# A mixer, its queries and its expert rows: running the second block's latents by tiles of 128 instead of both tiles at once

## The chip, the core and the metric

The kernel runs on one core of one Trainium2 chip. All data is float32. The metric is the device time of one execution in microseconds (us); lower is better. The engines are TensorE (PE, with its weight loads as PEld), VectorE (DVE), ScalarE (ACT), GpSimd (POOL) and SyncE (SP), each with a queue of its own that runs in order.

## What is computed

Two transformer blocks run one after the other on 256 tokens of width 1024, two tiles of 128 tokens. The second takes the first one's output as its "latents" and has 256 context tokens beside them (tiles 2 and 3). It has two layers: an even one (latent attention with 8 heads over context and latents, and a short convolution) and an odd one (4 heads of an mLSTM). After either mixer stands a layer of looked-up experts:

```python
def peer(h, w_q, subkeys, u, v):            # for each block of 128 tokens
    q = (xb @ w_q).reshape(128, 8, 2, 128)   # w_q: 1024 x 2048
    s = einsum('thpd,hpkd->thpk', q, subkeys)
    s1, i1 = top_k(s[:, :, 0], 16); s2, i2 = top_k(s[:, :, 1], 16)
    top, pos = top_k(all 256 sums of s1 and s2, 16); idx = i1 * 128 + i2 at pos
    g = softmax(top)
    ue, ve = u[idx], v[idx]                  # 8 heads x 16 rows of u and of v for every token
    return einsum('thk,thkd->td', g * gelu(einsum('td,thkd->thk', xb, ue)), ve)

# layer: x += gate * mixer(norm1(x)); x += gate * peer(norm2(x))
# layer 0 for context and latents, layer 1 for the latents alone
```

## The kernel before

Everything is written by hand: each engine has a program, a chain of Python generators, and waits on events of the others. What a program text says first, the engine does first.

**Expert rows.** For one tile, 128 times (8 heads by 16 picks) a row `x` is gathered: POOL issues one indirect DMA (L2111) that fetches, for each of 128 tokens, 2048 floats (a row of u and one of v), 1 MB. The tile pair makes 256 such rows. A row then passes DVE (the dot product with the token's normed vector, L2059), ACT (the gelu, a pair of rows at a time, L2024), DVE again (a diagonal matrix of the weights, L2054) and PE (four instructions of 128x512, L2012), and its buffer is free: only then may POOL issue the row that takes the buffer next. The text calls this the row's loop. There are three passes of 256 rows: the context's ("c", beside the first block and the latents' even mixer), the latents' of layer 0 ("l0") and of layer 1 ("l1"). The two latent passes have 11 buffers. DVE, in its spare time between dots, does the top sixteens: three instructions of them for every row (`rate` 3), 29 instructions for each of the 15 head-and-tile units left, so for the first 145 rows.

**Before the rows** stand, for the latents, the queries (`queries_pe`, L1930: weights of 256 columns as stationary blocks, both tiles' 256 tokens streamed past them, 8 pairs of blocks; L1941: the scores against the subkeys, 128 wide) and before them a norm and the mixer's tail: attention units and the output projection (L690), whose result DVE and POOL add to x (L1383, L1391). In layer 0 the tail has 16 units (8 heads by 2 tiles) and runs beside the end of the context's rows, and rows of layer 1's modulation (`more`; L324, L326, L339 on DVE, 16 pieces of 512 KB) are computed beside the queries. In layer 1 the tail has 8 units (4 heads by 2 tiles) and runs alone.

**Merging.** `merged(a, b)` advances two generators by declared shares: after a step of `a` with share s, steps of `b` with share `ROW` (0.47) are made until s is used up. This happens in each engine's program, so it sets one fixed order there.

```python
        def merged(a, b, due=0.0):
            for share in a:
                due += share
                while due > 0.0:
                    due -= next(b, 1.0e9)
            return due
```

Of the kernel before, what the change touches and what calls it, by code (L numbers as in the profile page):

```python
# [118 lines left out]
def program(nc, D, out):  # L119
    with ExitStack() as ctx:  # L120
# [93 lines left out]
        FIRST, SIX, PAIR = {0: (0, 1, 2, 3), 1: (0, 1, 2, 3, 4)}, (0, 1, 2, 3, 4, 5), (6, 7)  # L214
        BESIDE, SUMS = (4, 5, 6), (5, 6)
# [633 lines left out]
        CH, ROW, PACE = 0.45, 0.47, 0.8  # L849
# [576 lines left out]
        units2 = [(h, i) for h in range(8) for i in range(2)]  # L1426
# [5 lines left out]
        RINGS = {"c": BESIDE, "l": FIRST[1]}  # L1432

# [8 lines left out]
        def even_pe(pe, side):  # L1442
# [33 lines left out]
            for _ in lin_pe(pe, ("ukv", side), D["mla_w_ukv_2"][0], 1, (0, 1024), keys,  # L1476
                            lambda kc, t: kv_lhs(kc, t, tiles), seen=seen, ring=ring):
                pe.fill(1, side)
                yield CH
            nk = len(keys)  # L1480

            def s1(u):
                h, i = units2[u]
                if i == 0:
                    for n, src, m in (("q", b.Qh, 2), ("k", b.Kh, nk)):
                        flip_pe(pe, ("e" + n, side, h), [src[:, x, h, :] for x in range(m)], ring, ("rope2", side),
                                ("kr", side), [("ev", "lin", "uq", side, x, c) for x in tiles for c in (0, 512)],
                                [("ev", "lin", "ukv", side, x, c) for x in keys for c in (0, 512)])
                bk = bank(pe, ring, "esc", side, u)
                pe.wait_ge(("ev", "flip", "eq", side, h), ("ev", "flip", "ek", side, h))  # L1490
                pe.eng.matmul(bk[:, 0:128 * nk], b.QTE[h % 2][0:96, i * 128:(i + 1) * 128], b.KTE[h % 2][0:96, 0:128 * nk],
                              start=True, stop=True).then_inc(*pe.done("mm", "esc", side, u))

            def s2(u):
                bk = bank(pe, ring, "ept", side, u)
                pe.wait_ge(("ev", "esc", side, u))
                for x in range(nk):
                    ins = pe.eng.transpose(bk[:, x * 128:(x + 1) * 128], b.PB[u % 2][:, x * 128:(x + 1) * 128], ident)
                ins.then_inc(*pe.done("mm", "ept", side, u))

            def s3(u):
                h, i = units2[u]
                bk = bank(pe, ring, "eav", side, u)
                pe.wait_ge(("ev", "ept", side, u))
# [3 lines left out]
                ins.then_inc(*pe.done("mm", "eav", side, u))  # L1508

            for _ in stages(16, s1, s2, s3):  # L1510
                yield 0.5
            for t in tiles:
                turn_pe(pe, ("eo", side, t), b.O2[:, t - tiles[0], :], 4, ring,
                        [("eo", side, u) for u in range(16) if units2[u][1] == t - tiles[0]])
            seen = {t: turned_all(("eo", side, t), 4) + [("cy", side, 3)] for t in tiles}
            for _ in lin_pe(pe, ("eout", side), D["even_w_out_2"][0], 8, (0, 1024), tiles,
# [6 lines left out]
        def even_sp(sp, side):  # L1523
# [6 lines left out]
            for _ in range(18):  # L1530
# [8 lines left out]
        def even_act(a, side):  # L1539
# [49 lines left out]

            def s1(u):  # L1590
                h, i = units2[u]
                if i == 0:
                    copy_act(a, b.QTE[h % 2][0:96, :], psum("flip", "eq", side, h)[0:96, 0:256], ("mm", "flip", "eq", side, h),
                             ("mm", "esc", side, u - 3)).then_inc(*a.done("ev", "flip", "eq", side, h))
                a.wait_ge(a.last, ("enm", side, u), ("mm", "ept", side, u - 2))
                a.eng.activation(b.PB[u % 2][:, 0:128 * nk], psum("esc", side, u)[:, 0:128 * nk], ACT.Exp,
                                 bias=sm(1, "enm", u % 4), scale=96.0 ** -0.5, accum_out=sm(1, "esu", u % 4)).then_inc(
                    *a.done("ev", "esc", side, u))
# [1039 lines left out]
```

## Time and profile before

| | |
|---|---|
| median of 3 runs | 3900.23 us (3899.17 to 3910.28) |
| the profiled execution | 3910.66 us, span of its instructions 3909.4 us |
| PE busy | 3081.3 us, 79% of the span |
| DVE busy | 2423.5 us, 62% |
| POOL busy | 943.3 us, 24% |
| ACT busy | 809.2 us, 21% |
| moved by DMA | 1102 MB, mean 282 GB/s; of it 818.9 MB by the 768 gathers |
| mean granted clock of PE | 0.903 of 2.4 GHz |

The span can be read in stretches. Up to about 1990 us the first block, the context's whole layer 0 and the latents' even mixer run beside one another. From 1990 to 2125 us stand norm and queries of l0, then its 256 rows to about 2795 us. Then come the odd mixer's projections to 3001 us, its attention units to 3104 us, its output projection and norm to 3161 us, the queries of l1 to 3229 us, and its rows to the end.

### The profile page before, as it was taken

How to read it: one execution, taken by the hardware profiler on the slowest of the kernel's cores; microseconds unless marked ns; L12 is line 12 of the kernel's file. 1: busy time of each engine (PE TensorE's matmuls, PEld its weight loads, DVE VectorE, ACT ScalarE, POOL GpSimd, SP SyncE). 2: the span in 40 equal slices, each digit the busy share in tenths (PEclk: the TensorE clock that was granted, in tenths of full speed). 3: DMA queues.
4: the chain of work that ended last, by engine and by line, in shares of the span. 5: the costliest groups of instructions: out<-in, count | busy, mean ns of one | idle time of the engine just before them, and what ended most of it. 6: DMA issues, size and time to landing. Idle time of an engine off the chain costs nothing. (4 is left out here: it accounts for less than half of the span.)

```text
span 3909.4 us, 28560 instructions
## 1 busy us (share of the span) xinstructions
PE 3081.3 (79%) x8865; PEld 1611.0 (41%) x8865; DVE 2423.5 (62%) x5350; ACT 809.2 (21%) x1912; POOL 943.3 (24%) x842
## 2 busy tenths in 40 slices
PE   6899797899784689978777777777797796777776
PEld 1354464674332347635444222322343362222322
DVE  3124525886778856545655999866513518999665
ACT  1102232232323433223511111100101211111000
POOL 0000101222222222222211344433200014444432
PEclk7999898999896789989788999999996698999999
DMA  6665236999885679977555999999743039999998
GB/s 231 198 181 170 85 112 216 334 347 358 298 325 191 231 276 362 357 288 273 192 185 188 421 405 392 382 421 422 294 126 131 4 115 394 412 387 377 422 421 352
DMA packets 299625, 1102.17 MB, mean 282 GB/s; under 512 B 25588, under 2 KB 110272, under 8 KB 201168
## 3 DMA queue, kind: packets, MB, share of 16 engines
q0 software_dynamic: 114512, 818.87, 53.2%
q1 hardware_dynamic: 184336, 280.90, 21.7%
q8 instruction: 70, 1.15, 0.1%
q10 hardware_dynamic: 624, 0.57, 0.1%
q14 instruction: 83, 0.68, 0.0%
HBM read 1099.18 MB, written 1.05 MB: 281 GB/s over the span
## 5 line engine op out<-in xcount | busy, mean ns | idle before, releaser
L2012 PE MATMUL PS<-AR 128*128 128x512 f32 x2560 | 1256.2, 635 | 453.1 <-DVE AR L2054 351.9
L2111 POOL DMA_INDIRECT AR<-in_uv,AR x768 | 865.2, 1127 | 1713.4 <-PE PS L2012 1251.1
L2059 DVE CUSTOM_DVE_ANT_0 AR<-AR 128x1024 f32<-128x1024 f32 x768 | 935.4, 1220 | 293.8 <-DMA AR<-in_uv,AR 293.3
L2012 PEld LDWEIGHTS PS<-AR 128*128 128x128 f32 x2560 | 490.9, 200 | 1166.9 <-DVE AR L2054 546.0
L690 PE MATMUL PS<-AR 128*128 128x512 f32 (+3 forms) x1304 | 564.2, 587 | 37.0 <-DMA AR<-in_w_in 19.8
L2024 ACT ACTIVATE AR<-AR 128x2 f32<-128x2 f32 x384 | 78.1, 203 | 1479.7 <-DVE AR L2059 1478.7
L690 PEld LDWEIGHTS PS<-AR 128*128 128x128 f32 x1304 | 249.3, 204 | 324.7 <-issue 269.8
L326 DVE SCALAR_TENSOR_TENSOR AR<-AR,CC 128x512 f32<-128x512 f32 x280 | 210.5, 752 | 220.1 <-DMA AR<-in_w_ada 138.6
L987 PE MATMUL PS<-AR 128*128 128x256 f32 x1408 | 325.2, 390 | 21.9 <-DMA AR<-in_w_up_act 14.8
L987 PEld LDWEIGHTS PS<-AR 128*128 128x128 f32 x1408 | 274.5, 196 | 86.7 <-issue 20.6
L1930 PE MATMUL PS<-AR 128*128 128x256 f32 x768 | 189.2, 409 | 25.7 <-DMA AR<-in_peer_w_q 18.6
L2054 DVE TENSOR_SCALAR AR<-C,AR 128x128 f32<-128x128 f32 x512 | 156.6, 376 | 66.4 <-DVE AR L2059 48.6
L2024 ACT ACT_TABLE_LOAD x90 | 115.5, 1283 | 370.5 <-DVE AR L2059 370.5
L746 ACT ACTIVATE AR<-PS 128x256 f32<-128x256 f32 (+4 forms) x244 | 107.9, 442 | 372.8 <-PE PS L1930 160.1
L1930 PEld LDWEIGHTS PS<-AR 128*128 128x128 f32 x768 | 157.3, 208 | 52.4 <-DMA AR<-in_peer_w_q 19.4
L2047 DVE SCALAR_TENSOR_TENSOR AR<-AR 128x1024 f32<-128x1024 f32 x126 | 163.9, 1301 | 13.0 <-ACT AR L2035 8.6
L1001 PE MATMUL PS<-AR 128*128 128x512 f32 x352 | 154.7, 592 | 1.1 <-DVE AR L1221 1.1
L545 PE MATMUL PS<-C,AR 128*128 128x128 f32 x254 | 54.6, 385 | 114.9 <-DVE AR L629 65.4
L443 PE MATMUL PS<-AR,CC 128*2 128x512 f32 x192 | 93.1, 641 | 21.3 <-DMA AR<-in_w_mod 15.3
L1391 POOL TENSOR_TENSOR X<-X,AR 128x512 f32<-128x512 f32 x12 | 16.0, 1339 | 357.6 <-DVE AR L1383 357.6
L1001 PEld LDWEIGHTS PS<-AR 128*128 128x128 f32 x352 | 66.8, 190 | 85.6 <-issue 83.5
L545 PEld LDWEIGHTS PS<-C,AR 128*128 128x128 f32 x254 | 44.0, 201 | 132.1 <-DVE AR L629 66.1
(226 smaller groups left out, 2518.9 us busy)
## 6 DMA issues: line engine op xcount, KB each, us to landing
AR<-in_w_mod SPq DMA_DIRECT2D x96, 512.0 KB, 4.7
AR<-in_w_ada SPq DMA_DIRECT2D x96, 512.0 KB, 4.8
AR<-in_w_in SPq DMA_DIRECT2D x56, 512.0 KB, 4.1
AR<-in_peer_w_q SPq DMA_DIRECT2D x48, 512.0 KB, 3.5
AR<-in_w_up_act SPq DMA_DIRECT2D x44, 512.0 KB, 8.2
AR<-in_w_up_lin SPq DMA_DIRECT2D x44, 512.0 KB, 6.4
AR<-in_w_down SPq DMA_DIRECT2D x44, 512.0 KB, 6.6
AR<-in_even_w_in SPq DMA_DIRECT2D x24, 512.0 KB, 4.8
```

The lines of the kernel that those rows point to most:

```text
L326: v.eng.scalar_tensor_tensor(out=acc, in0=wt[:, c, :], scalar=col, in1=acc, op0=ALU.mult, op1=ALU.add).then_inc(*v.done(*end))
L690: ins = pe.eng.matmul(bk[:, 0:n], lhs(k0 + kc, t), wt[:, kc, :], start=(k0 + kc == 0), stop=(k0 + kc == nk - 1))
L746: return a.wait_ge(a.last, *events).activation(dst, src, ACT.Copy)
L987: ins = pe.eng.matmul(bk[:, f * 256:f * 256 + 256], wt[:, kc, cs], LAT.all[:, k0 + kc, :], start=(k0 + kc == 0 and f == 0), stop=(k0 + kc ...
L1001: ins = pe.eng.matmul(bs[t, hh], GT[:, f, t * 128:(t + 1) * 128], wt[:, 0, hh * 512:(hh + 1) * 512], start=(f == 0), stop=(f == 21))
L1930: ins = pe.eng.matmul(bk[:, f * 256:f * 256 + 256], wt[:, kc, cs], e.lay.all[:, k0 + kc, :], start=(k0 + kc == 0 and f == 0), stop=(k0 + k ...
L2012: ins = pe.eng.matmul(acc[i][hh], e.dg(x), e.buf(x)[:, 1024 + 512 * hh:1536 + 512 * hh], start=(x % 128 == 0), stop=(x % 128 == e.last))
L2024: a.eng.activation(hid, hid, ACT.Gelu).then_inc(*a.done("gelu2", e.key, x // 2))
L2047: v.eng.scalar_tensor_tensor(out=ACC, in0=row, scalar=w, in1=ACC, op0=ALU.mult, op1=ALU.add).then_inc(*v.done("sum", e.key, x))
L2054: v.eng.tensor_scalar(e.dg(x), ident, DT[x // 128][:, x % 128:x % 128 + 1], gw_at(x // 16, x % 16, 1), ALU.mult, ALU.mult).then_inc(*v.don ...
L2059: v.eng.tensor_tensor_reduce(e.buf(x)[:, 0:1024], e.buf(x)[:, 0:1024], norm2(e).H[e.tiles[x // 128]], 1.0, 0.0, ALU.mult, ALU.add, DT[x // ...
L2111: g.eng.indirect_dma_start(e.buf(x), None, D["uv"][e.l], bass.IndirectOffsetOnAxis(ap=idx_at(x // 16, x % 16, 1), axis=0)).then_inc(*land. ...
```

## The change

The latents of the second block no longer go through tail, queries and rows as a pair.

- The mixers' tails are functions of their own and take one tile: `even_tail_*(lane, "l0")` or `"l1"` with 8 units each, `odd_tail_*(lane, t)` with 4 units each. In both, a unit turns its head's keys anew: with two tiles apart every unit has its own key transposes and key copy.
- `queries` takes a list of tiles. For the latents it is run once for tile 0 and once for tile 1, so that the 8 MB of `peer_w_q` are read twice in each layer, and PE streams 128 tokens past each stationary block instead of 256.
- `second` sets the order: queries of tile 0, then the rows start; merged with them come tile 1's tail and tile 1's queries. In layer 0, `more` runs after that, one piece for each row.
- The row buffers: six until row 80, eleven after that. Tile 1's tail and queries use the memory of the other five.
- The sums of the rows have two PSUM banks (5, 6) instead of a ring of seven, so tile 1's first sum waits until tile 0's banks are read. The tails and queries have the rings (0 to 4), (0 to 3) and (4, 7).
- `ROW` is 0.45 instead of 0.47.
- The norm after the mixer is made for each tile by itself; for both tiles its shift is now added on DVE, where POOL had added tile 1's.

```diff
-        CH, ROW, PACE = 0.45, 0.47, 0.8
+        CH, ROW, PACE = 0.45, 0.45, 0.8
...
+        def query_tiles(e, ts):
+            w = 128 * len(ts)
+            base = ACC if ts[0] == 1 else SMALL[:, 768:1280]
+            return w, [base[:, w * i:w * i + w] for i in range(2)]
...
                             for kc in range(4):
-                                ins = pe.eng.matmul(bk[:, f * 256:f * 256 + 256], wt[:, kc, cs], e.lay.all[:, k0 + kc, :],
+                                ins = pe.eng.matmul(bk[:, f * w:f * w + w], wt[:, kc, cs], e.lay.all[:, k0 + kc, cols],
...
         def experts_pool(g, e):
-            g.wait_ge(("mm", "sco", e.key, 15), e.ready)
+            g.wait_ge(("mm", "sco", e.key, e.tiles[0], 15), e.ready)
             for st in range(e.steps):
                 if st < 256:
                     x, b = st, e.before[st]
                     g.wait_ge(("idx", e.key, x // 16), ("sum", e.key, b) if b is not None else None)
+                    if b is None and e.slot[x] in e.late:
+                        g.wait_ge(e.late_ready)
...
+        def odd_tail_pe(pe, t):
             def s1(u):
-                h, t = units3[u]
-                if t == 0:
-                    flip_pe(pe, ("oq", h), [Qp[:, i, h * 128:(h + 1) * 128] for i in range(2)], SIX,
-                            [("ev", "lin", "oq", x, 0) for x in range(2)])
-                    flip_pe(pe, ("ok", h), [Kp[:, i, h * 128:(h + 1) * 128] for i in FOUR], SIX,
-                            [("ev", "lin", "ok", x, 512) for x in FOUR])
-                bk = bank(pe, PAIR, "osc", u)
+                h = u % 4
+                flip_pe(pe, ("oq", u), [Qp[:, t, h * 128:(h + 1) * 128]], QUAD, [("ev", "lin", "oq", x, 0) for x in range(2)])
+                flip_pe(pe, ("ok", u), [Kp[:, i, h * 128:(h + 1) * 128] for i in FOUR], QUAD,
+                        [("ev", "lin", "ok", x, 512) for x in FOUR])
+                bk = bank(pe, LAST, "osc", u)
...
+        def staged(t, *parts):
+            for _ in stages(4, *[(lambda u, f=f: f(4 * t + u)) for f in parts]):
+                yield 1.5
...
-        WIDE = [0, 1, 2, 3, 4, 5, 8, 9, 10, 11, 12]
-        of_lat = [Experts(f"l{l}", l, [0, 1], LAT, 3, MAIN, HTt[:, 0:1024], WIDE, 0, 3, MAIN,
-                          mods.finished() + [("sum", before, 255)])
-                  for l, mods, before in ((0, more, "c"), (1, mods_of["odd"], "l0"))]
+        of_lat = [Experts(f"l{l}", l, [0, 1], LAT, 3, SUMS, HTt[:, 2048:3072], list(range(6)), 0, 3, FIRST[1], ready,
+                          [[0], [1]], late=[8, 9, 10, 11, 12], since=80, late_ready=after)
+                  for l, ready, after in ((0, [("sum", "c", 255)], res_x(("eout", "l1"), 1)),
+                                          (1, mods_of["odd"].finished() + [("sum", "l0", 255)], res_x(("oout", 1), 1)))]
...
+        def second(lane, l, tail, queries, experts, mods=None):
+            through(queries(lane, of_lat[l], [0]))
+            rows = experts(lane, of_lat[l])
+            merged(tail(lane, 1), rows)
+            merged(queries(lane, of_lat[l], [1]), rows)
+            lane.run(mods, "rows")
+            for _ in rows:
+                lane.fill(1, "rows")
+            lane.flush("rows")
...
-            merged(even(lane, "l"), beside, due)
+            due = merged(even(lane, "l"), beside, due)
+            merged(tail(lane, "l0"), beside, due)
             through(beside)
-            lane.run(more, "l0")
-            through(queries(lane, of_lat[0]))
-            lane.flush("l0")
+            second(lane, 0, lambda lane, t: tail(lane, f"l{t}"), queries, experts, more)
...
         def pe_program(pe):
             start_pe(pe)
-            both(pe, first_pe, even_pe, queries_pe, experts_pe)
-            through(experts_pe(pe, of_lat[0]))
+            both(pe, first_pe, even_pe, even_tail_pe, queries_pe, experts_pe)
             odd_pe(pe)
-            through(queries_pe(pe, of_lat[1]))
-            through(experts_pe(pe, of_lat[1]))
+            through(odd_tail_pe(pe, 0))
+            second(pe, 1, odd_tail_pe, queries_pe, experts_pe)
```

Three places of the order show what it does. On PE, at the queries of l1, the program had the queries of both tiles (L1930 256 wide; L1941 the scores) and, after the last of them, all sums of the rows (L2012):

```order
L1930 MATMUL PS<-AR 128x256 x16
L1941 MATMUL PS<-AR 128x128 x4
L1930 MATMUL PS<-AR 128x256 x16
L1941 MATMUL PS<-AR 128x128 x6
L2012 MATMUL PS<-AR 128x512 x512
```

In the changed kernel the second tile's queries (L1970, scores L1981) stand between the row sums (L2053, two of its matmuls for a row), here in layer 0 right behind the norm's transposes (L545):

```order
L545 MATMUL PS<-C,AR 128x128 x8
L1970 MATMUL PS<-AR 128x128 x16
L2053 MATMUL PS<-AR 128x512 x6
L1981 MATMUL PS<-AR 128x128
L2053 MATMUL PS<-AR 128x512 x4
L1970 MATMUL PS<-AR 128x128 x16
L1981 MATMUL PS<-AR 128x128
L2053 MATMUL PS<-AR 128x512 x4
L1981 MATMUL PS<-AR 128x128
L2053 MATMUL PS<-AR 128x512 x4
```

So each block of 16 query matmuls now stands behind four or five rows' sums, and the next sums stand behind it. On POOL, in layer 1, the residual sums (L1391), the subkey loads (L1994) and the gathers (L2111) were:

```order
L1391 TENSOR_TENSOR X<-X,AR 128x512 x4
L636 TENSOR_TENSOR AR<-AR,MOD 128x1024
L1994 DMA AR<-in_subk 128x4x128 x4
L2111 DMA AR<-in_uv,AR 128x2048 x256
```

and are now, with the subkey loads at L2035 and the gathers at L2153:

```order
L1391 TENSOR_TENSOR X<-X,AR 128x512 x2
L2035 DMA AR<-in_subk 128x4x128 x4
L2153 DMA AR<-in_uv,AR 128x2048 x28
L1391 TENSOR_TENSOR X<-X,AR 128x512
L2153 DMA AR<-in_uv,AR 128x2048 x4
L1391 TENSOR_TENSOR X<-X,AR 128x512
L2153 DMA AR<-in_uv,AR 128x2048 x2
L2035 DMA AR<-in_subk 128x4x128
L2153 DMA AR<-in_uv,AR 128x2048 x9
```

Two residual sums have come between the gathers, and each waits for a product that DVE makes behind the dots of the rows before. On DVE, the pieces of `more` in layer 0 (L324, L326), which stood beside the queries, are now between the dots (L2100), the diagonals (L2095) and the top sixteens (L1847 to L1916) of rows from about the sixtieth on:

```order
L326 SCALAR_TENSOR_TENSOR AR<-AR,CC 128x512 x4
L2095 TENSOR_SCALAR AR<-C,AR 128x128 x2
L2100 ISA AR<-AR 128x1024
L2100 ISA AR 128x1
L1856 MAX AR<-AR 128x8
L1859 MAX_INDEX AR<-AR 128x8
L1886 TENSOR_SCALAR AR<-AR 128x16
L326 SCALAR_TENSOR_TENSOR AR<-AR,CC 128x512 x4
```

One piece of four instructions has moved behind each row's dot and top sixteens.

## Rows read from the trace of the kernel before

**Rows 1.** The page, 40 equal slices of the span: busy tenths of DVE and DMA

```profile
DVE  3124525886778856545655999866513518999665
...
DMA  6665236999885679977555999999743039999998
```

**Rows 2.** Windows, busy time of each engine (instructions), granted clock, DMA share, GB/s

```profile
1855.00:1950.00 95.00, 67.00 (x292) 44.89 (x291) 60.74 (x119) 51.98 (x99) 23.29 (x18) 0.78 0.54 185
1990.00:2125.00 135.00, 99.37 (x373) 72.67 (x371) 70.72 (x117) 18.57 (x44) 7.10 (x8) 0.84 0.40 128
2125.00:2510.00 385.00, 277.66 (x557) 108.85 (x556) 353.66 (x969) 60.38 (x135) 166.17 (x149) 0.92 0.98 396
2510.00:2795.00 285.00, 217.35 (x470) 85.08 (x468) 176.05 (x346) 14.72 (x63) 105.95 (x109) 0.99 0.98 408
3001.00:3104.00 103.00, 78.29 (x168) 39.42 (x166) 58.52 (x172) 29.15 (x63) 0.00 (x0) 0.61 0.00 1
3104.00:3161.00 57.00, 37.09 (x97) 19.21 (x98) 16.44 (x25) 9.08 (x28) 8.89 (x7) 0.79 0.26 81
3161.00:3229.00 68.00, 66.37 (x320) 57.28 (x320) 9.30 (x34) 12.54 (x32) 1.54 (x3) 0.98 0.32 102
3229.00:3610.00 381.00, 273.08 (x547) 107.26 (x548) 350.81 (x963) 59.74 (x134) 166.79 (x147) 0.92 0.98 397
3610.00:3885.00 275.00, 208.53 (x455) 82.04 (x454) 173.18 (x341) 11.59 (x57) 108.27 (x111) 1.00 1.01 421
```

**Rows 3.** Timeline of POOL: first and last gather of l0, first of l1

```profile
2125.39 1.00 POOL L2111 DMA_INDIRECT AR<-in_uv,AR  x1 [25.79 <-PE PS L1941]
...
2769.22 0.94 POOL L2111 DMA_INDIRECT AR<-in_uv,AR  x1 [2.80 <-PE PS L2012]
...
3228.95 1.00 POOL L2111 DMA_INDIRECT AR<-in_uv,AR  x1 [25.36 <-PE PS L1941]
```

**Rows 4.** Waits, 2510 to 2780 us: us in total, times, longest

```profile
DVE AR L2059 <- DMA AR<-in_uv,AR: 79.0, 100, 1.3
```

**Rows 5.** Timeline of PE, 3119 to 3179 us: output projection, queries, scores

```profile
3119.62 29.27 PE L690 MATMUL PS<-AR 128*128 128x512 f32 x64
...
3177.48 1.41 PE L1941 MATMUL PS<-AR 128*128 128x128 f32 x8
3178.72 7.07 PE L1930 MATMUL PS<-AR 128*128 128x256 f32 x32
```

**Rows 6.** Weight loads of the l1 queries, 3161 to 3229 us: busy, mean ns

```profile
L1930 PEld LDWEIGHTS PS<-AR 128*128 128x128 f32 x256 | 49.1, 195 | 8.0 <-issue 1.4
```

**Rows 7.** Timeline of PE in l0's rows: the sums of two rows

```profile
2154.69 3.70 PE L2012 MATMUL PS<-AR 128*128 128x512 f32 x8 [2.02 <-DVE AR L2054]
```

**Rows 8.** Waits of DVE in the odd units, 3001 to 3104 us

```profile
DVE AR L2310 <- ACT AR L746: 35.0, 15, 4.8
DVE AR L749 <- PE PS L2185: 3.4, 1, 3.4
DVE AR L749 <- PE PS L574: 1.7, 1, 1.7
```

**Rows 9.** Waits of DVE in the even units, 1855 to 1950 us

```profile
DVE SM L1697 <- PE PS L1491: 23.8, 11, 3.0
```

**Rows 10.** DVE by line, 1990 to 2125 us: the modulation's pieces

```profile
L326 DVE SCALAR_TENSOR_TENSOR AR<-AR,CC 128x512 f32<-128x512 f32 x56 | 42.1, 752 | 7.5 <-DMA AR<-in_w_mod 5.6
L324 DVE TENSOR_SCALAR AR<-AR,CC 128x512 f32<-128x512 f32 x8 | 3.9, 486 | 6.6 <-PE PS L363 6.4
L339 DVE SCALAR_TENSOR_TENSOR MOD<-PS,MOD 128x512 f32<-128x512 f32 x4 | 2.8, 692 | 19.1 <-PE PS L363 19.1
```

**Rows 11.** Timeline of POOL, the odd mixer's residual sums of tile 0

```profile
3134.33 1.26 POOL L1391 TENSOR_TENSOR X<-X,AR 128x512 f32<-128x512 f32 x1 [307.15 <-DVE AR L1383]
```

**Rows 12.** The gathers, 2150 to 2480 us, from issue to landing

```profile
DMA to landing us min/median/max: 5.5/9.3/18.6
```

**Rows 13.** Windows: rows merged with the first block, columns as in rows 2

```profile
1300.00:1850.00 550.00, 473.25 (x1577) 300.37 (x1576) 322.18 (x551) 178.11 (x420) 144.17 (x122) 0.92 0.84 304
```

More of the change, by code:

```diff
@@ L1488, in s1 @@
                                 [("ev", "lin", "ukv", side, x, c) for x in keys for c in (0, 512)])
[L1489 to L1492, printed above, removed]
+                bk = bank(pe, ring, "esc", part, u)
@@ L1494, in s2 @@
+                pe.wait_ge(("ev", "flip", "eq", part, h), ("ev", "flip", "ek", part, h))
+                pe.eng.matmul(bk[:, 0:128 * nk], b.QTE[h % 2][0:96, at(i):at(i) + 128], b.KTE[h % 2][0:96, 0:128 * nk],
+                              start=True, stop=True).then_inc(*pe.done("mm", "esc", part, u))
             def s2(u):
-                bk = bank(pe, ring, "ept", side, u)
-                pe.wait_ge(("ev", "esc", side, u))
+                bk = bank(pe, ring, "ept", part, u)
+                pe.wait_ge(("ev", "esc", part, u))
@@ L1529, in even_sp, with even_tail_sp @@
                     yield CH
-            for _ in range(18):
+        def even_tail_sp(sp, part):
+            side = part[0]
+            for _ in range(len(UNITS[part]) + 2):
                 yield 0.5
@@ L1766, in program, with __init__ @@
         class Experts:
-            def __init__(self, key, l, tiles, lay, gate, banks, tmp, early, lag, rate, ring, ready, halved=False):
+            def __init__(self, key, l, tiles, lay, gate, banks, tmp, early, lag, rate, ring, ready, parts, halved=False, late=(), since=256,
+                         late_ready=()):
+                self.parts, self.late, self.late_ready = parts, late, list(late_ready)
                 self.halved = halved
@@ L1785, in __init__, with part, scored @@
                 self.slot, self.before, last_in = {}, {}, {}
-                free = list(early)
                 for x in range(256):
+                    free = list(early) + (list(late) if x >= since else [])
                     fresh = [i for i in free if i not in last_in]
-                    i = fresh[0] if fresh and x >= len(early) else (
-                        free[x] if x < len(early) else min(free, key=lambda i: last_in[i]))
+                    i = fresh[0] if fresh else min(free, key=lambda i: last_in[i])
                     self.slot[x], self.before[x] = i, last_in.get(i)
                     last_in[i] = x
+            def part(self, t):
+                return next(ts for ts in self.parts if t in ts)
+            def scored(self, t, u):
+                return ("ev", "sco", self.key, self.part(t)[0], u)
             def on_dve(self, x):
@@ L2081, in experts_dve @@
             todo = topk_all(v, e, 1, 16)
-            v.wait_ge([("ev", "sco", e.key, u) for u in range(16)])
             for st in range(e.steps):
@@ L2204, in odd_sp, with odd_tail_sp @@
             sp.flush()
-            for _ in lin(sp, 8, (0, 1024), [0, 1], nothing):
-                pass
+        def odd_tail_sp(sp, t):
+            yield from staged(t, nothing, nothing, nothing, nothing)
+            for _ in lin(sp, 8, (0, 1024), [t], nothing):
+                yield CH
+            yield 1.0
         def odd_act(a):
@@ L2493, in context @@
                 yield PACE * share
+            for share in tail(lane, "c"):
+                yield PACE * share
             lane.run(cgate, "c")
-            for share in queries(lane, of_ctx):
+            for share in queries(lane, of_ctx, [2, 3]):
                 yield PACE * share
@@ L2498, in context, with both @@
             yield from experts(lane, of_ctx)
-        def both(lane, first, even, queries, experts):
-            beside = context(lane, even, queries, experts)
+        def second(lane, l, tail, queries, experts, mods=None):
[7 more added lines that the diff above has]
+            lane.flush("rows")
+        def both(lane, first, even, tail, queries, experts):
+            beside = context(lane, even, tail, queries, experts)
             due = merged(first(lane, 0), beside)
```

364 lines of the change are left out of this document (189 added, 175 removed).

## The prediction

> **What bounds the kernel now.** I read the slices first [rows 1]: DMA is full in slices 22 to 29 and 33 to 40, the two latent passes, and nearly idle at slices 31 to 33, the odd mixer's tail. The windows give each stretch its limit [rows 2]. A pass has two parts. In the first 145 rows DVE also does the top sixteens: l0 takes 385 us, of which about 12 us are the start, so 373/145 = 2.57 us a row, with DVE busy 353.7 us (2.44 a row) and DMA at 0.98. DVE and DMA are both at their limit. In the other 111 rows DVE is busy 62% and PE 76%, DMA alone sets the pace at 2.5 us a row, and DVE waits for it 100 times [rows 4]. In l1 the same numbers return. Between the passes stand stretches in which no row moves: 1990 to 2125 us, and 3001 to 3229 us. The gathers start at 2125.4 and 3229.0 us [rows 3].
>
> The change shortens these stretches and puts what it takes out into the first 62 rows of each pass. (Tile 1's tail and queries declare shares of 9.6 and 18 in layer 0, 9 to 11 and 18 in layer 1; over 0.45 this is about 20 and 40 rows, of which the order shows 61 or 62.) Those rows are the ones where DVE has nothing to spare. So the question is how much DVE time was idle in what is removed, and how much new waiting DVE gets.
>
> **What is removed from in front of the rows.**
>
> Layer 1. Attention: 8 units took 103 us [rows 2]; four take four steps of about 12 and the same filling and draining, some 60: −43. Output projection: 64 instructions in 29.3 us [rows 5], half of it −15. Scaling and squares of four heads fewer: −3. Queries: a pair of blocks took 7.07 + 1.41 us [rows 5]. For 128 tokens the nearest row is the score's, the same shape with a stationary block of its own: 8 instructions in 1.41 us, 0.176 each. A pair is then 32 + 4 of them, 6.3 us, not half of 8.5: the weight loads, 195 ns [rows 6], no longer hide behind a stream of 221 ns. Eight pairs and 2 us around them make 52 us for 68: −16. Sum −77.
>
> Layer 0. The tail runs beside the last context rows. Its step took 95/16 = 5.9 us with one row in it [rows 2]; ten steps for 18, each now with key transposes and a key copy, say 6.5: −35. Projection and residual −10. The new `ROW` moves ten context rows ahead, into a stretch where PE is busy 86% [rows 13]; I charge 15. Norm and queries took 135 us with `more` beside them, now 14 + 52: −69. Sum −99.
>
> Together **−176**.
>
> **What is added to the rows.**
>
> Queries of tile 1, in either layer: PE does 40 rows at 1.85 [rows 7] and 8 pairs at 6.3, 125 us. Rows merged with other PE work kept PE busy 86% [rows 13], so 145 us where 40 rows took 103: +42 each. If PE were never idle it would be +22; that is the lower bound.
>
> Layer 1's tail: DVE's work for four units is 58.5/2 = 29, two key copies 1.4, and the norm side half of 16.4 plus a shift of 1.2 that POOL did: +40 in all [rows 2]. DVE's waits come along, since its queue is in order and dots stand behind them. In each unit it waits for ACT's copy of a PSUM bank that PE fills only after DVE's own key copy: 35.0/2 = 17, draining 5 [rows 8]; root of the squares, transposes and norm, estimated from the same stretch's idle DVE, 8. The two residual sums are new waits on POOL: it holds the next gathers until DVE has made the product [rows 11], so DVE finds no landed row and waits out 1.3 us of adding and 5.5 us of the shortest landing [rows 12], 7 each: 14. Sum +84.
>
> Layer 0's tail: 10 steps with 11 rows in them. The step of before plus a key flip and a whole row's sum on PE instead of half is 7.5: 75 us for 28, +47. DVE's waits there were for scores, up to 3.0 us each [rows 9]. Projection: PE 14.6 + 8 rows of 1.85 = 29, at 86% 34 us for 21: +13. Residual sums beyond that +7, norm +7. Sum +74.
>
> `more`: 42.1 + 3.9 + 2.8 = 49 us of DVE [rows 10]. It was hidden beside the queries, where DVE was half idle. Now it stands behind rows 62 to 79, which still carry top sixteens, so all of it counts: +49. Spread over the last 111 rows it would have cost nothing.
>
> Small ones: sums of tile 1 wait for tile 0's banks, +4 a pass; the 12 us start of a pass is in part covered, −5 a pass; DMA carries some 16 MB more, in rows where it now has room, 0. After a wait DVE finds rows landed and works at 2.44 instead of 2.57: 124 rows by 0.13, −16.
>
> Sum: layer 1 84 + 42 − 1 = 125; layer 0 74 + 42 + 49 − 1 = 164; less 16: **+273**. Against −176 this is +97, on the profiled execution's 3910.7 us 4008; the median of the runs was 10 us below it: **3997, say 4000 us**.
>
> **Rivals.**
>
> 1. *It overlaps as meant.* No waits of DVE beyond its work: layer 1's tail +40, layer 0's about +30 (60.7 us of DVE there over 16 steps, less its rows), queries +22 each, `more` +49, less 16: +147 against −176, **3871 us**. For it: PE is a few us ahead of DVE at each step's start, since the last diagonal is one to two rows old. Against it: the ACT waits of [rows 8] arise from DVE's own copy, so no lead helps. It decides at one number: with `more` fixed at 49, the rows 0 to 61 of both passes may take (176 − 49)/124 = 1.02 us more than 2.57, so below 3.6 us a row the kernel is faster. I expect 4.4. Chance 0.12.
>
> 2. *The six buffers set the pace.* A row's loop is issue 1, landing 5.5, its dot and three top sixteens 2.4, the partner's dot and diagonals 2.2, the sum 1.85: 13 us, over 6 buffers 2.2 us a row, under 2.57. But each block of 5.6 us on PE and each wait of DVE lies in the loop once or twice; where both do, 6 rows take over 30 us, 5.2 a row. Over 124 rows that is 0.8 us a row more than forecast, **4100 us**. The median landing of 9.3 us [rows 12] speaks for it, though there 11 buffers queue up. Chance 0.13.
>
> 3. *Nothing measurable*, between 1 and the forecast, **3900 us**: the units' waits fall where rows are late anyway. Chance 0.07.
>
> 4. *The narrow query matmuls cost half.* If 16 of them took 7.07/2 us, a pair would be 4.2: 2.1 less, 33 us over the serial 16 pairs and about 40 over the merged ones, **3927 us**. Against it stands the score's row at the same width, 0.176 a piece. Chance 0.03. The Trainium skill goes further: its page "TensorE: Matmul & The Clock Gate", section "Back-to-back issue gap", gives some 81 ns for a pair of weight load and 128-wide matmul, and "LDWEIGHTS (loading the stationary operand)" 107 ns for 128 columns. By that the pair of blocks would be 2.9 us and the kernel would come out near 3865. This trace does not agree for float32: 176 ns between instructions, 195 ns for a load.
>
> The forecast itself, a slower kernel by some 60 to 150 us, has 0.65.
>
> **How the numbers follow.** A measurement of this kernel tells about 0.3% (12 us) from no change. Faster: rival 1 and a little of 4, 0.13. Same: 0.08. Slower: the rest, 0.79. The range goes from the sum without any waiting, 3875, up to rival 2's, 4100: 3875 to 4100 leaves out some 0.15. The forecast's own range is 3950 to 4060.
>
> **What would show it.** The first gather of l0 near 2030 us, that of l1 some 151 us behind the start of the odd units instead of 228. Then 60 rows at 4 to 4.6 us each, with DMA at 0.6 and DVE at 0.75; DVE waiting for ACT copies, for PE's scores and, at two places in a pass, 7 us for a gather. In the queries' rows PE busy 85% or more and each 16 matmuls near 5.6 us. In l0's rows 62 to 79, 5.3 us a row. From row 145 on 2.5 us as before. A first stretch under 3.6 us a row would make the prediction wrong; so would `more` running beside landed rows without lengthening them, or query matmuls of 0.11 us.

## The result

| | median (lowest to highest, runs) |
|---|---|
| before | 3905.26 us (3899.17 to 3912.38, 4) |
| after | 3963.67 us (3961.41 to 3978.71, 4) |

The ratio is 1.0157, with a 95% interval of 1.0124 to 1.019: the change makes the kernel 58 us slower. The profiled execution of after took 3978.71 us, 68 more than that of before and 15 above after's median, so the two executions read below differ by 10 us more than the medians do. The slices of after's page, each 99 us, against [rows 1]:

```profile
span 3977.4 us, 29933 instructions
DVE  3124426896768756554556888866513376799665
PEclk7999898999986789989788969999996778999999
DMA  6665236998985689977568969999733357999998
```

The l0 pass now begins in slice 21, but with 6 and 8 tenths of DMA, and has a hole (6 tenths) in slice 24; l1 begins in slice 33 with 5 and 7. Windows of after, in the order of the program (rows with tail, with queries, with `more`, the last 111 rows; then l1's tail and queries). Columns as in [rows 2]:

```profile
2011.00:2134.00 123.00, 83.93 (x261) 44.53 (x259) 77.77 (x202) 32.08 (x62) 31.63 (x28) 0.81 0.67 245
2134.00:2274.00 140.00, 116.11 (x461) 69.87 (x462) 107.79 (x286) 29.70 (x77) 51.80 (x46) 0.92 0.94 367
2274.00:2393.00 119.00, 78.61 (x99) 25.75 (x99) 93.99 (x193) 9.96 (x21) 24.71 (x21) 0.67 0.69 264
2560.00:2835.00 275.00, 207.29 (x448) 81.05 (x447) 169.86 (x333) 11.19 (x55) 102.27 (x105) 0.99 1.00 417
3187.00:3372.00 185.00, 118.01 (x267) 54.05 (x268) 128.18 (x344) 42.60 (x91) 43.49 (x40) 0.79 0.65 237
3372.00:3501.00 129.00, 110.91 (x448) 66.14 (x448) 103.59 (x279) 25.71 (x69) 44.54 (x43) 0.94 0.96 372
```

In the tail's rows no engine is near its limit (DVE 63 and 69%, DMA 0.67 and 0.65): they are rows of waits. With the queries DMA is at 0.94 to 0.96 and PE at 83 and 86%. With `more` DVE is busy 79% and DMA a third idle. The last rows are as before.

The balance, by the times between the dots of two rows. Gain: the first dot of l0 stands at 2017.6 us instead of 2131.0, −113.4, and from l0's last dot to l1's first it is 363.8 us instead of 445.5, −81.7; −195 in all. Loss: l0's pass takes 817.2 instead of 658.2 us (+159), l1's 761.8 instead of 657.7 (+104); +263. The difference is the +68.

This table is worked out from the timelines: us from the dot of one row to that of another, for all kernels. The first number is l0's, the second l1's; a pass goes from the dot of row 0 to that of row 255.

| kernel | rows 0–34 | 34–62 | 62–80 | 80–145 | 145–255 | pass |
|---|---|---|---|---|---|---|
| before | 93, 92 | 77, 77 | 49, 49 | 167, 167 | 273, 273 | 658, 658 |
| after | 165, 173 | 91, 95 | 119, 52 | 167, 167 | 274, 275 | 817, 762 |
| e1 | 167, 173 | 91, 96 | 49, 51 | 167, 167 | 294, 275 | 768, 762 |
| e2 | 167, 175 | 92, 95 | 116, 54 | 155, 162 | 277, 277 | 806, 764 |
| e3 | 89, 90 | 68, 67 | 46, 46 | 164, 164 | 277, 277 | 644, 644 |
| e4 | 111, 113 | 82, 80 | 50, 50 | 222, 167 | 266, 275 | 731, 685 |
| e5 | 98, 97 | 79, 79 | 50, 51 | 167, 167 | 272, 273 | 666, 667 |
| e6 | 160, 179 | 94, 92 | 119, 50 | 167, 167 | 275, 275 | 814, 763 |
| e7 | 157, 164 | 90, 96 | 119, 51 | 167, 167 | 274, 275 | 807, 753 |
| e8 | 150, 166 | 92, 96 | 43, 43 | 160, 157 | 302, 277 | 748, 740 |
| e9 | 166, 174 | 86, 90 | 119, 51 | 167, 167 | 274, 275 | 812, 757 |
| e10 | 143, 162 | 74, 77 | 46, 43 | 164, 161 | 303, 277 | 729, 720 |
| e11 | 135, 138 | 98, 108 | 74, 73 | 157, 156 | 297, 276 | 760, 750 |

The first dot of l0 stands between 2003 and 2031 us in the kernels whose program is the same up to there, so single profiles differ by up to 28 us ahead of the rows; where that matters, the passes are compared. Within a pass, rows 0 to 22 of l1 took 100.8 us in after and 104.2 and 104.3 in e6 and e2, whose edits begin later: 3 us in one cell of the table is no difference.

### The profile page after: what moved, and what is told of

It reads as the page before. It is cut to its first block and busy times, and to the rows that moved or that the text cites. A ratio compares the mean times of both kernels' runs of the same rounds, so it can differ in the third digit from the quotient of the medians.

```text
span 3977.4 us, 29933 instructions
## 1 busy us (share of the span) xinstructions
PE 3119.6 (78%) x9425; PEld 1652.0 (42%) x9425; DVE 2443.9 (61%) x5365; ACT 832.1 (21%) x1999; POOL 951.1 (24%) x848
## 5 line engine op out<-in xcount | busy, mean ns | idle before, releaser
L2053 PE MATMUL PS<-AR 128*128 128x512 f32 x2560 | 1274.8, 641 | 381.0 <-DVE AR L2095 294.4
L2153 POOL DMA_INDIRECT AR<-in_uv,AR x768 | 870.9, 1134 | 1862.1 <-PE PS L2053 1383.9
L2100 DVE CUSTOM_DVE_ANT_0 AR<-AR 128x1024 f32<-128x1024 f32 x768 | 936.1, 1222 | 353.9 <-DMA AR<-in_uv,AR 352.7
L2053 PEld LDWEIGHTS PS<-AR 128*128 128x128 f32 x2560 | 499.1, 204 | 1076.3 <-issue 495.6
L690 PE MATMUL PS<-AR 128*128 128x512 f32 (+3 forms) x1304 | 575.5, 593 | 46.3 <-DMA AR<-in_w_in 20.0
L690 PEld LDWEIGHTS PS<-AR 128*128 128x128 f32 x1304 | 252.0, 207 | 339.0 <-issue 281.0
L326 DVE SCALAR_TENSOR_TENSOR AR<-AR,CC 128x512 f32<-128x512 f32 x280 | 210.6, 752 | 217.1 <-DMA AR<-in_w_ada 138.3
L987 PE MATMUL PS<-AR 128*128 128x256 f32 x1408 | 324.7, 389 | 17.2 <-DMA AR<-in_w_up_act 12.2
L987 PEld LDWEIGHTS PS<-AR 128*128 128x128 f32 x1408 | 273.2, 195 | 84.0 <-issue 21.3
L2095 DVE TENSOR_SCALAR AR<-C,AR 128x128 f32<-128x128 f32 x512 | 161.2, 382 | 76.1 <-DVE AR L2100 48.3
L1970 PE MATMUL PS<-AR 128*128 128x128 f32 (+1 forms) x1280 | 193.2, 313 | 11.0 <-ACT AR L746 3.8
L746 ACT ACTIVATE AR<-PS 128x128 f32<-128x128 f32 (+6 forms) x316 | 120.2, 380 | 360.6 <-PE PS L1970 142.6
L545 PE MATMUL PS<-C,AR 128*128 128x128 f32 x254 | 53.4, 377 | 179.3 <-DVE AR L629 124.2
L1970 PEld LDWEIGHTS PS<-AR 128*128 128x128 f32 x1280 | 180.5, 206 | 29.0 <-issue 12.5
L1001 PE MATMUL PS<-AR 128*128 128x512 f32 x352 | 154.7, 592 | 1.1 <-DVE AR L1221 1.1
L545 PEld LDWEIGHTS PS<-C,AR 128*128 128x128 f32 x254 | 42.7, 196 | 196.5 <-DVE AR L629 133.0
L1001 PEld LDWEIGHTS PS<-AR 128*128 128x128 f32 x352 | 66.8, 190 | 85.2 <-issue 83.5
L1391 POOL TENSOR_TENSOR X<-X,AR 128x512 f32<-128x512 f32 x12 | 16.2, 1354 | 342.8 <-DVE AR L1383 342.8
```

The costliest lines, as they stand in the source:

```text
L326: v.eng.scalar_tensor_tensor(out=acc, in0=wt[:, c, :], scalar=col, in1=acc, op0=ALU.mult, op1=ALU.add).then_inc(*v.done(*end))
L690: ins = pe.eng.matmul(bk[:, 0:n], lhs(k0 + kc, t), wt[:, kc, :], start=(k0 + kc == 0), stop=(k0 + kc == nk - 1))
L746: return a.wait_ge(a.last, *events).activation(dst, src, ACT.Copy)
L987: ins = pe.eng.matmul(bk[:, f * 256:f * 256 + 256], wt[:, kc, cs], LAT.all[:, k0 + kc, :], start=(k0 + kc == 0 and f == 0), stop=(k0 + kc ...
L1001: ins = pe.eng.matmul(bs[t, hh], GT[:, f, t * 128:(t + 1) * 128], wt[:, 0, hh * 512:(hh + 1) * 512], start=(f == 0), stop=(f == 21))
L1970: ins = pe.eng.matmul(bk[:, f * w:f * w + w], wt[:, kc, cs], e.lay.all[:, k0 + kc, cols], start=(k0 + kc == 0 and f == 0), stop=(k0 + kc = ...
```

## The experiments

Ratios are to runs of the kernel before on the same chip, with a 95% interval. "After" is the changed kernel.

**e1: `more` one piece to every fourth row, in rows 154 to 214** (`st` counts the rows left behind the queries, 62 fewer than the row's number).

```diff
-            for _ in rows:
-                lane.fill(1, "rows")
+            for st, _ in enumerate(rows):
+                if st >= 92 and st % 4 == 0:
+                    lane.fill(1, "rows")
```

> The changed kernel, but in layer 0 the 16 pieces of the modulation `more` are computed beside rows of the last part of the pass, one piece for every fourth row from about row 155 on, instead of one for each of the rows 62 to 79. Theory A (DVE has nothing to spare in the first 145 rows, and has 0.9 us a row to spare in the last 111): the rows 62 to 80 of layer 0, which took 119 us against 49 in the kernel before, go back to about 49, and the last part of the pass grows by under 10 us; the kernel is 60 to 70 us faster than the changed one, about 3900, as fast as the kernel before or a little faster. Theory B (the slow rows 62 to 80 come from the six row buffers and not from the pieces): these rows stay near 110 us, and the time stays within 15 us of the changed kernel's 3964.

Measured: 3929.28 us, ratio 1.0056 [1.0038, 1.0075], 34 us under after in the median and 48 in the profile, where theory A has 60 to 70. Rows 62 to 80 fell from 119 to 49 us, the time of before: `more` had cost 70 there, more than the 49 of the sum. So A is right there, and B is wrong. But rows 145 to 255 took 294 us, 20 more and not the under 10 of theory A. Windows of e1, at rows 62 on and in the last rows:

```profile
2340.00:2395.00 55.00, 39.31 (x82) 15.54 (x83) 51.69 (x143) 9.38 (x21) 21.70 (x21) 0.97 1.01 421
2560.00:2700.00 140.00, 111.52 (x230) 43.33 (x229) 110.29 (x202) 7.47 (x29) 59.84 (x50) 0.95 1.02 418
```

DVE is busy 79% in the last rows and hides `more`; DMA is at 1.02. The pieces are 16 of 512 KB, 8.4 MB, and at 421 GB/s they take 20 us. Here work moved into rows that wait for DMA was free on DVE, not in bytes.

**e2 and e3: two top-sixteen steps in a row instead of three, from row 24,** in after (e2) and in before (e3).

```diff
+            def pace(self, st):
+                return 2 if not self.halved and st >= 24 else self.rate
-                for _ in range(e.rate):
+                for _ in range(e.pace(st)):
```

> The changed kernel, but both latent passes do three instructions of the top sixteens a row only for the first 24 rows and two a row after that. Theory A (DVE bounds the merged rows and those up to 145): each row from 24 to 145 gives back up to 0.34 us of DVE, so merged rows and the rows up to 145 get faster until DMA at 2.5 us a row bounds them: 10 to 25 us a pass, 3915 to 3945. The rows 145 to 205 carry the rest of the top sixteens in DVE's spare time and stay at 2.5 us. Theory C (waits for other engines and not DVE's work bound the merged rows): under 10 us in all, 3955 to 3965.

> The kernel before with the same slower pace of the top sixteens. Theory A: the rows 24 to 145 go from 2.57 to DMA's 2.5 us, so 5 to 10 us a pass, 3880 to 3895. If DMA alone had been the bound there, no change.

Measured: e2 3973.07 us, 1.0165 [1.0133, 1.0196], no gain; e3 3881.43 us, 0.9944 [0.9923, 0.9965], 22 us less than before. In before, rows 34 to 62 fell from 77 to 68 us, 2.43 a row, so DVE's work had been above DMA's there (theory A, with more than its 5 to 10 us a pass: 14). In after the same rows stayed at 92: with a third less top sixteens they are not shorter, so the work of DVE was not alone in setting them. Rows 80 to 145 of e2's l0 did get faster, by 12 us; in l1 by 5.

**e4: e1 with tile 1's tail and queries run ahead of the rows, still in parts of one tile.**

```diff
-            merged(tail(lane, 1), rows)
-            merged(queries(lane, of_lat[l], [1]), rows)
+            through(tail(lane, 1))
+            through(queries(lane, of_lat[l], [1]))
```

> The changed kernel with the late modulation of e1_more_late, and with tile 1's tail and queries in front of the rows, not merged with them: only the split by tiles is left, and all the rows run undisturbed. Against e1: the passes should take some 640 us again (86 us less in layer 0, 104 us less in layer 1), and in front of the rows the tile's tail and queries stand alone, some 110 to 130 us in each layer. Theory A: 25 to 70 us slower than e1, about 3925 to 3970, so the merging itself gains a little and what it gains is smaller than the 200 us that it hides, because DVE's and PE's work comes back in the rows. Theory D (the merging loses): this kernel is faster than e1.

Measured: 4031.8 us, 1.0335 [1.0304, 1.0365], 103 over e1. The first dot of l0 comes 93 us later than in e1, and l1's gap grows by 120 us (484 for 364). The merging itself wins: 213 us of serial time for 115 us of rows (l1's pass falls by 77, l0's by 38). Of these 98 us some 27 are not the merging's: with no rows used up ahead of it, the same line puts `more` into rows 92 to 152, beside top sixteens, and rows 80 to 255 take 488 us for e1's 461. Theory A had the direction, and 25 to 70 us for the measured 103. What is lost against before is the splitting: l1's gap in e4 is 38 us longer than before's 445.5, and rows 0 to 34 take 111 and 113 us instead of 93. The trace shows why these rows are slower. The gathers may start when tile 0's scores are in, so the first six go out before the last query weights of tile 1 (l0 of e4, PE, then DVE's waits over rows 1 to 34, in both layers the same 17.0 us):

```profile
2119.42 3.53 PE L1970 MATMUL PS<-AR 128*128 128x128 f32 x16 [8.56 <-DMA AR<-in_peer_w_q]
2126.27 3.52 PE L1970 MATMUL PS<-AR 128*128 128x128 f32 x16 [3.31 <-DMA AR<-in_peer_w_q]
...
DVE AR L2095 <- ACT AR L2065: 17.9, 2, 17.0
```

PE waits for the weights, ACT's copy of the scores waits for PE, the gelu of the first row pair stands behind it, and DVE waits 17.0 us for that. Six buffers add 5 (e5); together this is the 19 to 20 us.

**e5 and e6: the six buffers.** e5 is before, with its rows up to 80 on six buffers; e6 is after, with the other buffers from row 24 (l0) and 36 (l1) instead of 80, and this is its edit:

```diff
-                          [[0], [1]], late=[8, 9, 10, 11, 12], since=80, late_ready=after)
+                          [[0], [1]], late=[8, 9, 10, 11, 12], since=(24, 36)[l], late_ready=after)
```

> The kernel before, but both latent passes use only six row buffers until row 80, as the changed one does; nothing is merged with the rows. Theory E (the six buffers by themselves slow the rows, apart from what is merged): as in the unmerged passes of e4_serial, the rows 0 to 80 take about 243 us instead of 218, so 25 us a pass and 50 us in all, 3945 to 3960. Theory F (a row's loop of 13 us over six buffers is short enough, and e4's slower start had another cause): under 15 us in all, up to 3918.

> The changed kernel, but the five later row buffers are used from row 24 on in layer 0 and from row 36 on in layer 1, right behind tile 1's tail, instead of from row 80 on. Theory E: the rows from there to 80 are the queries' rows, which cost 20 to 24 us more a pass than before; with eleven buffers they give back 10 to 20 us a pass, so 3925 to 3945, and rows 62 to 80 of layer 0 change too. Theory F: PE's query matmuls and DVE's waits for other engines set the pace there whatever the buffers are; under 10 us in all, 3954 to 3964.

Measured: e5 3931.78 us, 1.007 [1.0048, 1.0092], +28; e6 3969.77 us, 1.017 [1.0142, 1.0199], the same as after. In e5 the passes grow by 8 and 10 us, all of it in rows 0 to 74, about 0.12 us a row: neither E's 25 a pass nor F's under 15 in all. Of the 28 us, 5 lie outside the passes in the profile and 5 are the difference between medians and profiled executions; no run says more of them. DVE's waits over the first 156 us of e5's pass:

```profile
DVE AR L2060 <- DMA AR<-in_uv,AR: 9.6, 13, 4.4
```

It waits 13 times for a row: 4.4 us at the first one, 5.2 in the other 12. Before has 5.5 us in 2 such waits there. In e6 rows 22 to 34 of l0 gain 6 us and rows 34 to 62 lose 3; the passes are the same within 3 us (theory F). Six buffers cost something, and not what a pass loses. The two PSUM banks for the sums cost no more: e4, which has them, takes 82 and 80 us for rows 34 to 62, e5, which has seven, 79 and 79.

**e7: the two residual sums beside the rows made by DVE itself instead of POOL.**

```diff
+                if key in BESIDE_ROWS:
+                    v.wait_ge(v.last)
+                    v.eng.tensor_tensor(Xt[:, t, c0:c0 + n], Xt[:, t, c0:c0 + n], res_tmp(tmp, i), ALU.add).then_inc(
+                        *v.done("summed", *key, i))
```

> The changed kernel, but the two residual sums of tile 1 in each layer are made by DVE right behind its product, so that POOL's gathers no longer wait for DVE there. The trace of the changed kernel shows DVE waiting 6.5 and 5.6 us for a gather behind the two sums of layer 0. Theory G (the gathers held back behind the sums cost what DVE waits): some 6 us back for each of four sums, less 0.7 us of DVE each, so 15 to 22 us, 3942 to 3949. Theory H (the next rows wait anyway, for the transposes or PE's sums): under 5 us.

Measured: 3960.0 us, 1.0146 [1.012, 1.0173], 4 under after in the median and 13 in the profile. The intervals of the two overlap, so the total alone decides nothing; the passes do. After's timeline at the first of these sums shows what it takes away (start us, length, engine, line, idle before and what ended it):

```profile
2099.59 1.26 POOL L1391 TENSOR_TENSOR X<-X,AR 128x512 f32<-128x512 f32 x1 [8.95 <-DVE AR L1383]
2101.01 1.00 POOL L2153 DMA_INDIRECT AR<-in_uv,AR  x1 [0.15 <-issue]
...
2107.66 1.23 DVE L2100 CUSTOM_DVE_ANT_0 AR<-AR 128x1024 f32<-128x1024 f32 x1 [6.46 <-DMA AR<-in_uv,AR]
```

POOL stood 8.95 us for DVE's product, added, and only then issued the gathers of the next rows; DVE stood 6.5 us for one. DVE's waits of e7 over rows 0 to 34 of l1, against after's 17.1 us in 6 for the gathers (below):

```profile
DVE AR L2109 <- DMA AR<-in_uv,AR: 8.4, 5, 3.6
```

In l1 DVE's waits for gathers fell by 9 us, and the passes by 10 and 9 (theory G has 15 to 22 for both together, and these are 19).

**e8: all four edits (e1, e2, e6, e7) in after.**

> The changed kernel with all four edits: late modulation (e1), slower pace of the top sixteens (e2), later buffers from rows 24 and 36 (e6), residual sums on DVE (e7). If the costs add: 35 to 40 us from e1, 15 to 20 from e7, 20 to 40 from e6, and with more buffers the slower top sixteens count in the merged rows too, 10 to 20: 3860 to 3885, as fast as e3_before_rate (3881) or a little faster, so that the split by tiles would be worth 0 to 20 us over a kernel with the same pace of the top sixteens. If the waits of DVE's queue in tile 1's tail stay as they are, no more than that.

Measured: 3882.25 us over 10 runs, 0.9948 [0.9929, 0.9967]: 81 under after, 22 under before, and level with e3, which is before with one of the four edits. With the four edits the change is worth nothing against a before with one of them: against e3 it starts l0 112 us earlier and closes the gap to l1 from 448 to 360 us, and pays 104 and 96 us in the passes. The waits of e8 from 2200 to 2258 us, the second part of rows 34 to 62, on all engines:

```profile
ACT AR L746 <- PE PS L1982: 27.3, 3, 12.3
...
DVE AR L2107 <- ACT AR L2077: 13.2, 3, 9.3
...
PE PS L1982 <- DMA AR<-in_peer_w_q: 9.8, 2, 8.1
```

A chain through three queues: PE stands at a query matmul (L1982) whose weights have not landed; ACT stands at its copy (L746); the gelu of a row pair (L2077) is behind that copy in ACT's queue; DVE needs it for a diagonal (L2107). The weights share the DMA engines with the rows in flight:

```profile
AR<-in_peer_w_q SPq DMA_DIRECT2D x6, 512.0 KB, 20.6
```

The median from issue to landing is 20.6 us here, over the whole of after 4.9. It is not the eleven buffers that do this: in after's rows with queries, on six buffers, the median of its 12 loads is 21.5 us.

**e9 and e10: a quarter of tile 1's query weights loaded,** in after (e9) and in e8 (e10). Tile 1's queries, and so the rows that it gathers, are then not the reference's; the number of gathers is.

```diff
-            sp.eng.dma_start(view(RAW, i * 1024, nk, nw), src).then_inc(
+            k1 = 1 if thin else nk
+            sp.eng.dma_start(view(RAW, i * 1024, nk, nw)[:, 0:k1, :], src[:, 0:k1, :]).then_inc(
```

> The changed kernel, but of each query weight chunk of tile 1 only the first of its four parts of 128 KB is loaded (the matmuls read what stands in the buffer, so tile 1's queries are not the reference's). It takes 12.6 MB of transfer out of the two passes and no instruction of PE, DVE or ACT. Theory G: in the rows that are merged with the queries the transfers are the bound (DMA at 0.94 from 2134 to 2274 us, and a chunk lands 21.5 us after its issue, 4.9 elsewhere), so each pass gets shorter by what its 6.3 MB take at 2.43 us a MB, 15 us, 30 in all: about 3934 us. Theory H: the six buffers and DVE's and PE's waits are the bound there, the transfers only look busy because requests queue: under 8 us in all, 3956 or more.

> The same on the kernel with all four edits, where the trace has DMA at 1.02 in the rows with the queries. Theory G: 30 us less than that kernel, about 3852 us. Theory H: 3874 or more. If the kernel with four edits gains the 30 and the plain changed kernel doesn't, the top sixteens' rate was the bound of the latter.

Measured: e9 3957.59 us, 1.0136 [1.0112, 1.016], 6 under after; e10 3852.15 us, 0.9857 [0.9834, 0.9879], 30 under e8 in the medians and the profile, what theory G gives; the passes fell by 19 and 20 us where G has 15 each. The windows of rows 34 to 62 in e8 and of rows 35 to 67 in e10, one below the other:

```profile
2166.00:2258.00 92.00, 74.44 (x297) 46.13 (x296) 60.54 (x158) 14.65 (x44) 39.42 (x30) 0.91 1.02 397
```
```profile
2166.00:2250.00 84.00, 78.94 (x312) 45.21 (x311) 69.56 (x181) 17.70 (x49) 44.34 (x34) 0.97 1.02 414
```

Rows 34 to 62 fell from 92 to 74 and from 96 to 77 us. PE's waits for query weights, 17.6 us from 2166 to 2258 us in e8, are gone in e10, and PE is busy 94% of its window. So in e8 three quarters of the second reading of the query weights cost 19 us of what these rows take beyond e3's 68 and 67; the other 5 and 10 stay.

In after itself it hardly does (−5 us a pass): the rows stay at 3.1 to 3.2 us. What holds them there is not shown. e10 differs from e9 in the rate of the top sixteens, and also in having eleven buffers in these rows, and no run has one without the other; by themselves neither gained anything (e2, e6). Nor does the DMA share tell: in e9's rows 34 to 62 it is still 0.99, at 385 GB/s, though three quarters of these bytes are gone.

**e11: e8 with the tail spread to row 50.**

```diff
-            merged(tail(lane, 1), rows)
+            merged((share * (2.3, 1.5)[l] for share in tail(lane, 1)), rows)
```

(and the other five buffers, which the expectation counts as seven, from rows 54 and 56)

> The kernel with all four edits, but the tail of tile 1 is laid over more rows: its shares are multiplied by 2.3 in layer 0 and 1.5 in layer 1, so that it ends near row 50 in both instead of 21 to 34, and the queries near row 90; the seven more buffers come into use from row 54 and 56. Theory J: DVE's waits in the tail are hidden as soon as there are more rows beside each, since rows 0 to 34 take 150 and 166 us there where DVE and DMA need about 85 for the rows: 25 us a pass less, about 3832 us. Theory K: each wait stands in DVE's queue with no landed work ahead of it, however few there are in a row, so the sum is the same: 3882 us, within 10. The longer use of six buffers costs 3 to 5 us a pass in either.

Measured: 3906.43 us over 12 runs, 0.9992 [0.9976, 1.0009], 24 over e8 (17 by the ratios). Rows 0 to 34 fell by 16 and 28 us, rows 34 to 80 rose by 37 and 41. Theory J is wrong. K's sum of waits is the nearer, but it had 3882 within 10, and the pass did not stay the same: it grew by 12 and 11 us where 3 to 5 was expected. Here the thinner tail moved its waits along; why it added to them is not separated from the longer use of six buffers, nor from `more`, which now lies in rows 182 to 242.

## Why the prediction was right, and where its terms were off

The likeliest case came true: the units' waits, DVE's narrow margin and `more` cost more than the serial time saved. The sum was 4008 us on the profiled execution, measured 3978.71; +97 became +68. That it came so near is in part luck: by the table, queries beside the rows cost 40 us less than forecast, layer 0's tail 12 and layer 1's 3 less and the serial part 19 less, and `more` cost 22 more, while the 16 us of catch-up can't be seen.

**Removed, layer 1, −77:** from the last gather of l0 to the first of l1 it is 459.7 us before and 372.6 after, −87. The first gather of l1 stands 137 us behind the first scores of the attention units (3187.0 and 3049.8 us); by the same mark it was 226 before, and −77 would have made it 149. **Layer 0, −99:** −114.5 by the first gather (2125.4 and 2010.9 us). Up to the context's last row it was −31, as the −35, −10 and +15 give; but ten steps of 6.5 us for eighteen of 5.9 are −41, not −35: by its own terms the prediction should have taken off 6 us more here. Norm and queries gave −83.5 instead of −69.

**The price of a pair of blocks, 6.3 us, is the term that failed.** It measured 4.5. After's timeline in the serial queries:

```profile
1978.44 3.74 PE L1970 MATMUL PS<-AR 128*128 128x128 f32 x32
1982.93 3.74 PE L1970 MATMUL PS<-AR 128*128 128x128 f32 x32
```

32 instructions take 3.74 us, 0.117 each, about half of the wide one's 7.07/32 [rows 5], and pair follows pair after 4.49 us. I had taken 0.176 from the eight scores, which are no stream. Eight pairs at 4.5 instead of 6.3 are 14.5 us less, all that layer 0's −83.5 has over −69. The groups of 2134 to 2274 us say why the loads are no obstacle:

```profile
L1970 PE MATMUL PS<-AR 128*128 128x128 f32 x256 | 33.9, 297 | 0.9 <-issue 0.9
L1970 PEld LDWEIGHTS PS<-AR 128*128 128x128 f32 x256 | 33.9, 214 | 4.9 <-issue 4.9
```

256 loads of 214 ns each would be 55 us one after the other, but lie in 33.9 us of busy time: they overlap one another. The Trainium skill, page "TensorE: Matmul & The Clock Gate", section "Back-to-back issue gap", gives some 81 ns for load and matmul; the trace has 117 ns for float32, so it is nearer to the page than to my 176. This is rival 4, to which I gave 0.03, and the prediction had named matmuls of 0.11 us as a sign of being wrong. As a mechanism rival 4 came true, and its gains came too: 29 us by eight serial pairs in each layer (forecast 33), 40 beside the rows (forecast 40). Its time of 3927 is about as far off as the forecast's, since `more` and the missing catch-up took 38 of these 69 us back. By the page's 81 ns the prediction's own way of counting gives some 3880, not the 3865 that it states.

**Queries of tile 1 beside rows, +42 each:** rows 22 to 62 of l0 took 24 us more, rows 34 to 74 of l1 20 more. With the measured pair the forecast's own formula gives this: 40 rows of 1.85 and 8 pairs of 4.5 are 110 us of PE, at 86% 128 us, +25. PE was busy 83 and 86% there. That is worked out; no run takes PE's part alone away. The bytes I had put at nothing ("in rows where it now has room, 0"), and they are not nothing: DMA was at 0.94 to 0.96, to leave out three quarters of them gave 5 us a pass in after (e9) and 19 to 20 in e8 (e10). All 8.4 MB at 421 GB/s would be 20 us. So PE's share, and which of the two limits holds after's rows, stay open.

**Layer 1's tail, +84:** +81. **Layer 0's tail, +74:** rows 0 to 22 took +62. The waits are those named. After, DVE, rows 0 to 34 of l1:

```profile
DVE AR L2100 <- DMA AR<-in_uv,AR: 17.1, 6, 5.5
DVE AR L2359 <- ACT AR L746: 16.6, 8, 4.4
DVE SM L623 <- ACT SM L613: 4.4, 1, 4.4
DVE AR L562 <- PE PS L545: 4.3, 2, 2.1
```

16.6 us for ACT's copies of the bank (forecast 17, with another 5), 17.1 for gathers (forecast 14 for the two residual sums; 10.8 are the first waits behind them, and e7 took 9 away), 8.7 for the norm (forecast 8). The text of the prediction put this tail at about 20 rows by its shares; it covers 34, as the order of the gathers in POOL's program already showed, so the loss lies in rows 0 to 34, and tile 1's queries lie in rows 34 to 74. The size did not hang on that. Of the 143 us of both tails runs took away 19 (e7), and with no tail merged rows 0 to 34 take 111 and 113 us (e4); how the rest divides into DVE's work and its other waits is read from the trace.

**`more`, +49:** +71, 6.6 us a row for the forecast 5.3. DVE's 49 us lost their cover as said, but waits came along, 15 us of them for PE's part of it. After, DVE, 2300 to 2380 us:

```profile
DVE MOD L339 <- PE PS L363: 10.2, 4, 4.2
DVE AR L324 <- PE PS L363: 4.9, 2, 3.5
```

PE's granted clock was lower there (last section): two L363 took 2.07 us, where before's took 1.12 beside the queries. How much of the waits that makes, no run separates. DMA fell to 0.69. That it "would have cost nothing" over the last 111 rows is wrong by 20 us, the time of its bytes (e1).

**Rows 0 to 61** took 4.1 us each in l0 and 4.3 in l1, forecast 4.4, break-even 3.6. **Rival 1** (3871) fell by this; e8 shows that even with the four edits the merged rows do not reach it, and get 3882. **Rival 2**, the six buffers: e5 prices them at 8 to 10 us a pass, not 50, and e6, with eleven in most of the merged rows, is no faster than after. **The slices:** DMA is full in slices 23 to 28 and 34 to 39 [rows 1], one or two fewer than the prediction reads; nothing rests on them. **The catch-up of −16** lies in the same rows as the waits and can't be told from them.

## What to carry to other kernels

In this kernel, work that was moved out of the serial part cost beside other work what it did not overlap: its waits in an in-order queue, and its bytes where the rows were bound by DMA. Before counting a cover as free, ask it of each resource apart: DVE's time for `more` was free in the last rows, its 8.4 MB were not. A price for an instruction should come from a stream of it, not from a handful. Splitting by tile reads the weights twice, and here that gave nearly nothing: from l1's first query matmul to its first gather it is 39.8 us for 68.1, 28 saved, and the same queries cost 20 to 24 beside the rows. And give the kernel before the same tuning as the kernel after: one edit in before (e3) won as much as the whole change with four.

## What the runs showed of the hardware

- Float32 matmuls of 128x128 by 128 columns with a new stationary block each follow at 117 ns (32 in 3.74 us), those of 256 columns at 221 ns (32 in 7.07 us [rows 5]): half the width at about half the price, both at a granted clock of 1.00. The 32 narrow ones took 6.54 us at 2140 us, where the granted clock was 0.57 and PE had stood 14.3 us waiting for DVE.
- Small transfers among the gathers: at a DMA share of 1.01 to 1.02 the kernel moved 397 GB/s with the query weights (mean packet 1.2 KB) among them (e8), 414 with a quarter of them (e10), 421 without (e1). A 512 KB transfer then lands 20.6 us after its issue, where the median over after is 4.9.
- PE's granted clock was 0.67 on average in the rows with `more` (PE busy 66% there), after 0.92 in the 140 us ahead of them, at 83%. Its full level is 2.4 GHz, its lower one 1.2. The sums of two rows took 6.2 to 6.7 us in windows at 0.56 to 0.61, for 3.7 at the full clock.
